# One-hot arrays of the expert routing: from whole-group two-array operations to per-query one-array operations on fixed engines

## The reference, cut to what matters

```python
q = (x @ w_pq).reshape(N, PEER_HEADS, 2, PEER_DQ_HALF)
s1 = einsum('nhd,kd->nhk', q[:, :, 0], k_sub1)      # 8 heads x 128 keys
s2 = einsum('nhd,kd->nhk', q[:, :, 1], k_sub2)
v1, i1 = top_k(s1, 16);  v2, i2 = top_k(s2, 16)
cand = v1[..., :, None] + v2[..., None, :]
sc, pos = top_k(cand, 16)
idx = take_along_axis(i1 * 128 + i2, pos)
wts = softmax(sc)
...
act = gelu(einsum('nhed,nd->nhe', u_exp[idx], x))
out = einsum('nhe,nhed->nd', wts * act, v_exp[idx])
```

## Time and profile before

| what | value |
|---|---|
| median of three runs | 5878.06 us |
| the profiled execution's own time | 5881.79 us |
| its span, first to last instruction | 5880.2 us |
| mean granted TensorE clock | 0.94 |
| TensorE busy | 5142.8 us (87%) |
| VectorE busy | 3439.7 us (58%) |
| ScalarE busy | 1786.7 us (30%) |
| GpSimd busy | 1495.8 us (25%) |
| compares on VectorE, L1933 | 48, 83.9 us |
| GpSimd's subtractions, L1786, and multiplies, L1797 | 48 each, 115.0 and 105.6 us |
| ScalarE's Abs, L1879, and Relu, L1883 | 48 each, 50.8 and 50.7 us |

### The profile page before, as it was taken

The page is one execution under the profiler, slowest core; times in us unless marked ns, Lnnn a source line. Parts: engine busy times, 40 slices in busy tenths (PEclk is TensorE's granted clock), DMA queues, the critical chain, the costliest instruction groups (busy, mean ns, idle before and its releaser), DMA issues. The chain is left out here.

```text
span 5880.2 us, 62559 instructions
## 1 busy us (share of the span) xinstructions
PE 5142.8 (87%) x23461; PEld 4166.5 (71%) x23461; DVE 3439.7 (58%) x4209; ACT 1786.7 (30%) x2132; POOL 1495.8 (25%) x1065
## 2 busy tenths in 40 slices
PE   8979999999998787989694449999999999978884
PEld 3347888888876334877573439999999899957673
DVE  7832211117663332222318777888888778878888
ACT  7743121222212111122314633333333223323332
POOL 0300000000000331000204642333333333344553
PEclk9989999999999898989896769999999999999997
DMA  9832322232323554432511449999999999999997
GB/s 357 308 129 92 107 98 87 96 109 99 111 81 117 176 199 148 159 110 84 161 65 49 101 134 362 386 367 384 373 379 380 369 373 377 377 383 408 402 410 312
DMA packets 467404, 1355.44 MB, mean 231 GB/s; under 512 B 137468, under 2 KB 194812, under 8 KB 383918
## 3 DMA queue, kind: packets, MB, share of 16 engines
q1 hardware_dynamic: 340500, 677.84, 32.8%
q0 software_dynamic: 99616, 633.82, 27.5%
q10 hardware_dynamic: 27072, 40.91, 2.0%
HBM read 1216.48 MB, written 137.04 MB: 230 GB/s over the span
## 5 line engine op out<-in xcount | busy, mean ns | idle before, releaser
L227 PE MATMUL ps<-w_hi,act_hi 128*128 128x512 f32 x3040 | 1196.8, 394 | 41.9 <-DVE act_lo L1032 23.0
L228 PE MATMUL ps<-w_lo,act_hi 128*128 128x512 f32 x3040 | 1191.1, 392 | 0.0
L229 PE MATMUL ps<-w_hi,act_lo 128*128 128x512 f32 x3040 | 1190.2, 392 | 0.0
L222 DVE TENSOR_TENSOR w_lo<-w_stage,w_hi 128x2048 fp32r<-128x2048 f32 x152 | 348.3, 2292 | 1270.3 <-ACT w_hi L218 1268.5
L2229 ACT ACTIVATE x_hi<-x_stage 128x1024 fp32r<-128x1024 f32 x512 | 543.5, 1061 | 1509.1 <-DMA x_stage<-u_turned 720.9
L2309 DVE TENSOR_TENSOR x_lo<-x_stage,x_hi 128x1024 fp32r<-128x1024 f32 x512 | 625.3, 1221 | 373.9 <-ACT x_hi L2229 369.4
L2156 POOL DMA_INDIRECT u_ring<-u_exp,idx_all x256 | 597.2, 2333 | 892.1 <-DVE u_ring L2327 833.3
L2183 PE MATMUL ps<-act_hi,x_hi 128*128 128x384 f32 x2048 | 697.8, 341 | 70.6 <-DVE x_lo L2309 67.9
L2183 PE MATMUL ps<-x_hi,cx_hi 128*128 128x512 f32 x1536 | 612.4, 399 | 101.0 <-DVE cx_lo L2320 84.1
L218 ACT ACTIVATE w_hi<-w_stage 128x2048 fp32r<-128x2048 f32 x152 | 291.1, 1916 | 1335.4 <-PE ps L229 1301.1
L2184 PE MATMUL ps<-act_lo,x_hi 128*128 128x384 f32 x2048 | 694.9, 339 | 0.0
(11 more groups left out here) (296 smaller groups left out, 5954.6 us busy)
## 6 DMA issues: line engine op xcount, KB each, us to landing
x_stage<-u_turned SPq DMA_DIRECT2D x256, 512.0 KB
x_stage<-v_exp SPq DMA_DIRECT2D x256, 512.0 KB
w_stage<-w_ada SPq DMA_DIRECT2D x96, 1024.0 KB, 6.1
w_stage<-w_in SPq DMA_DIRECT2D x96, 1024.0 KB, 5.2
d_w<-w_buf SPq DMA_DIRECT2D x6, 4096.0 KB, 20.7
gwr<-d_w SPq DMA_DIRECT2D x128, 192.0 KB
d_gw<-gob ACTq DMA_DIRECT2D x128, 192.0 KB
gwr<-d_gw SPq DMA_DIRECT2D x128, 192.0 KB
```

The source lines that it names most:

```text
L222: dve.tensor_tensor(w_lo[:, q % 2], w_in_st[:, q], w_hi[:, q % 2].bitcast(F32), ALU.subtract).then_inc(w_split, 1)
L227: pe.matmul(out, lhs[0], rhs[0], start=first, stop=False)
L228: pe.matmul(out, lhs[0], rhs[1], start=False, stop=False)
L229: return pe.matmul(out, lhs[1], rhs[0], start=False, stop=last)
```

## The change

An operation now makes the one-hot of a single token: `tensor_scalar` compares the numbers 0 to 127 (one array of 128 columns) with a number a partition, and for the second array multiplies by another number a partition. A group is 8 such calls. Who makes it is fixed by group number: of four groups, the first array is made by ScalarE, ScalarE, VectorE, GpSimd, the second by GpSimd, VectorE, VectorE, VectorE. Where ScalarE makes the first array it does eight Abs calls of 128 columns with the key as bias, and one Relu on 1024 columns. The subtraction and the multiplication on GpSimd are gone, with their semaphores; each engine has a semaphore of its own for the groups that it makes. one2's ring has four groups now, one1's still three. pij and pf are placed in an area that was free, dist has one buffer.

```diff
-    RING = 3
+    RING1, RING2 = 3, 4
     half = 4 * TT * KD * P
     spare = 4 * ND * KD * P
+    FIRST_BY = ("act", "act", "dve", "pool")
+    SECOND_BY = ("pool", "dve", "dve", "dve")
+
+    def makers(table, Q):
+
+        who = table[Q % len(table)]
+        return who, sum(table[n % len(table)] == who for n in range(Q + 1))
+
     at_sb = nc.alloc_sbuf_tensor_at
     qt = at_sb("qt", [P, NH, P], F32, offset=area + spare)
     q_t = at_sb("q_t", [P, NH, P], F32, offset=area + spare + 4 * NH * P)
     hot = at_sb("hot", [P, PH, TOPK, TOPK], F32, offset=area + half + spare)
-    dist = at_sb("dist", [P, 2, 8, P], F32, offset=area + half + spare + 4 * NH * P)
+    dist = at_sb("dist", [P, 8, P], F32, offset=area + half + spare + 4 * NH * P)
+    pij = at_sb("pij", [P, 4, PH, TOPK], U32, offset=area + half + spare + 4 * NH * P + 32 * P)
+    pf = at_sb("pf", [P, 4, PH, TOPK], F32, offset=area + half + spare + 4 * NH * P + 48 * P)
...
-        one1 = sb(st, "one1", [P, RING, 8, P])
-        one2 = sb(st, "one2", [P, RING, 8, P])
+        one1 = sb(st, "one1", [P, RING1, 8, P])
+        one2 = sb(st, "one2", [P, RING2, 8, P])
...
-        id_ready, id_taken, s_diff, s_dist, s_one1, s_eq2, s_one2 = (
-            sem("r_" + n) for n in ("idready", "idtaken", "diff", "dist", "one1", "eq2", "one2"))
+        id_ready, id_taken, s_dist = (sem("r_" + n) for n in ("idready", "idtaken", "dist"))
+        s_one1 = {who: sem("r_one1" + who) for who in ("act", "pool", "dve")}
+        s_one2 = {who: sem("r_one2" + who) for who in ("pool", "dve")}
...
-        def key_pairs(t, n, q):
-
-            return (iota.unsqueeze(1).broadcast_to([P, 8, P]),
-                    id_t[:, t % 2, n, 8 * q:8 * q + 8].unsqueeze(2).broadcast_to([P, 8, P]))
+        def first_hot(eng, who, Q):
+
+            if Q >= RING1:
+                eng.wait_ge(w_ready, 2 * (Q - RING1) + 2)
+            t, q = divmod(Q, NQ)
+            for j in range(8):
+                n = 8 * q + j
+                made = eng.tensor_scalar(one1[:, Q % RING1, j], iota, id_t[:, t % 2, 0, n:n + 1], None, ALU.is_equal)
+            made.then_inc(s_one1[who], 1)
+
+        def second_hot(eng, who, Q):
+
+            if Q >= RING2:
+                eng.wait_ge(w_ready, 2 * (Q - RING2) + 2)
+            t, q = divmod(Q, NQ)
+            for j in range(8):
+                n = 8 * q + j
+                made = eng.tensor_scalar(one2[:, Q % RING2, j], iota, id_t[:, t % 2, 1, n:n + 1],
+                                         id_t[:, t % 2, 2, n:n + 1], ALU.is_equal, ALU.mult)
+            made.then_inc(s_one2[who], 1)
...
-            def differ(t, q):
-                Q = t * NQ + q
-                if Q >= 2:
-                    pool.wait_ge(s_one1, Q - 1)
-                pool.tensor_tensor(dist[:, Q % 2], *key_pairs(t, 0, q), ALU.subtract).then_inc(s_diff, 1)
-
             for t in range(ND):
                 pool.wait_ge(id_taken, t + 1)
                 for q in range(NQ):
                     Q = t * NQ + q
-                    if q == 0:
-                        differ(t, 0)
-                    if q < NQ - 1:
-                        differ(t, q + 1)
-                    pool.wait_ge(s_eq2, Q + 1)
-                    pool.tensor_tensor(one2[:, Q % RING], one2[:, Q % RING],
-                                       id_t[:, t % 2, 2, 8 * q:8 * q + 8].unsqueeze(2).broadcast_to([P, 8, P]),
-                                       ALU.mult).then_inc(s_one2, 1)
+                    if makers(SECOND_BY, Q)[0] == "pool":
+                        second_hot(pool, "pool", Q)
+                    if makers(FIRST_BY, Q)[0] == "pool":
+                        first_hot(pool, "pool", Q)
...
-                pe.wait_ge(s_one1, Q + 1)
-                pe.wait_ge(s_one2, Q + 1)
+                who, made = makers(FIRST_BY, Q)
+                pe.wait_ge(s_one1[who], made)
+                who, made = makers(SECOND_BY, Q)
+                pe.wait_ge(s_one2[who], made)
                 for h in range(2):
                     G = 2 * Q + h
                     if G >= 2:
                         pe.wait_ge(w_taken, G - 1)
                     for j in range(4):
-                        mm = pe.matmul(ps[:, 6 + G % 2, j * P:(j + 1) * P], one1[:, Q % RING, 4 * h + j],
-                                       one2[:, Q % RING, 4 * h + j], start=True, stop=True)
+                        mm = pe.matmul(ps[:, 6 + G % 2, j * P:(j + 1) * P], one1[:, Q % RING1, 4 * h + j],
+                                       one2[:, Q % RING2, 4 * h + j], start=True, stop=True)
...
-                act.wait_ge(s_diff, Q + 1)
-                act.activation(dist[:, Q % 2], dist[:, Q % 2], ACT.Abs).then_inc(s_dist, 1)
-                act.wait_ge(s_dist, Q + 1)
-                if Q >= RING:
-                    act.wait_ge(w_ready, 2 * (Q - RING) + 2)
-                act.activation(one1[:, Q % RING], dist[:, Q % 2], ACT.Relu, scale=-1.0, bias=1.0).then_inc(s_one1, 1)
+                who, made = makers(FIRST_BY, Q)
+                if who != "act":
+                    return
+                if made > 1:
+                    act.wait_ge(s_one1["act"], made - 1)
+                for j in range(8):
+                    n = 8 * q + j
+                    act.activation(dist[:, j], iota, ACT.Abs, scale=-1.0,
+                                   bias=id_t[:, t % 2, 0, n:n + 1]).then_inc(s_dist, 1)
+                act.wait_ge(s_dist, 8 * made)
+                if Q >= RING1:
+                    act.wait_ge(w_ready, 2 * (Q - RING1) + 2)
+                act.activation(one1[:, Q % RING1], dist[:], ACT.Relu, scale=-1.0, bias=1.0).then_inc(s_one1["act"], 1)
...
                     t, q = divmod(Q, NQ)
                     if q == 0:
                         dve.wait_ge(id_taken, t + 1)
-                    if Q >= RING:
-                        dve.wait_ge(w_ready, 2 * (Q - RING) + 2)
-                    dve.tensor_tensor(one2[:, Q % RING], *key_pairs(t, 1, q), ALU.is_equal).then_inc(s_eq2, 1)
+                    if makers(FIRST_BY, Q)[0] == "dve":
+                        first_hot(dve, "dve", Q)
+                    if makers(SECOND_BY, Q)[0] == "dve":
+                        second_hot(dve, "dve", Q)
```

More of the change, by code:

```diff
@@ L1733, in route @@
         pos = sb(st, "pos", [P, PH, TOPK], U32)
-        pij = sb(st, "pij", [P, 4, PH, TOPK], U32)
-        pf = sb(st, "pf", [P, 4, PH, TOPK])
         step1 = sb(st, "step1", [P, PH, TOPK])
```

## The result

| what | before | after |
|---|---|---|
| median of seven runs (lowest to highest), us | 5867.74 (5855.97 to 5882.37) | 5834.27 (5829.05 to 5848.73) |
| ratio, 95% interval | | 0.9946 [0.9929, 0.9963] |
| routing, first MAX8 of tile 0 to SyncE's first load behind the stage, us | 396.1 (3103.07 to 3499.18) | 363.8 (3098.63 to 3462.44) |
| VectorE busy in that time, us | 342.1 | 326.4 |

About 32 us faster at the ratio's middle, 0.54%. The forecast was 5870 with a range from 5842: too high, and the faster rival (5843) came in, nearly 9 us beyond its own number. Of the 36 us between 5870 and 5834, 10 lie in the starting point: the forecast was counted from the 5878.06 of three runs, and seven runs of the kernel before give 5867.74. The rest is the change itself, forecast at 9 us and measured at 32. The two profiled executions lie 52.7 us apart (5881.79 and 5829.05).

The account below looks back on a forecast made before the run. VectorE's own program with its waits was taken to bound routing. Tiles 1 and 2 at 97.8 us against 102.5 and tile 3 at 93.5 against 93.0 gave -9 us together, 5870 us at the median; range 5842 to 5905.

Parts of the forecast that it names:

- the faster rival: GpSimd's 128-column calls hardly cost VectorE the port in routing: stalls about 4 us a tile, -35 us, 5843; chance 0.33.
- What bounds the kernel: Routing lasts as long as VectorE's own program with its waits; a microsecond on that path is one of the kernel.
- (1): VectorE in routing: 16 compares removed, -18.2 us a tile.
- (2): VectorE in routing: 12 second and 4 first groups of 8 small calls added, 31.4 us a tile.
- (3): VectorE's waits for spreading matmuls, exponential and tail: 5.8 us a tile instead of 19.0; tile 3, 1.3 instead of 7.4.
- (4): GpSimd gets 64 one-array calls a tile, taken at 0.50 us each: 32 us of work against 61 before.
- the slower rival: GpSimd's small calls are nearly all fixed cost, 0.8 to 0.9 us: at 0.92, +46 us, 5924; chance 0.23.
- d: The length of one GpSimd 128-column one-array call in routing, taken as 0.50 us; break-even at 0.57.
- S: VectorE's port stalls a tile in routing; the change is 3S-47 us and breaks even at S = 15.7.
- (5): VectorE's port stalls beside GpSimd's calls: 10.8 us plus 2 for hot operations, 12.8 us a tile instead of 17.5 to 19.4.
- (6): ScalarE's eight groups of Abs calls and a Relu take 29 us a tile against 34, and cost nothing.
- 43 pairs: The count per tile of VectorE small calls meeting a GpSimd call in routing, at 0.25 us each: 10.8 us.

Follow-up runs that it names:

- kernel 4: The changed kernel with GpSimd's groups made by VectorE too, so that GpSimd makes none: 5855.44 us, 0.9979.
- kernel 9: The changed kernel with group 12's second array made by VectorE and group 11's first by ScalarE: 5847.04 us, 0.9963.
- kernel 3: The kernel before, its VectorE compare made by eight one-number calls of 128 columns a group, GpSimd's two-array operations kept: 5888.0 us, 1.0029.
- kernel 2: The changed kernel with GpSimd's share made by two-array calls of 128 columns (its output is not one-hot): 5842.09 us, 0.9949.
- kernels 1 and 8: 1: kernel before, GpSimd's operations one-array, 512 columns, half of each group omitted, 5813.77 us; 8: changed kernel, earlier exponential, two group arrays moved, VectorE first arrays two-array, 5815.04 us.
- kernel 7: The changed kernel with ScalarE's exponential for the next tile issued behind the eviction of group 11 instead of group 13: 5813.41 us, 0.9904.

## Why the prediction was wrong, step by step

- **What bounds the kernel:** right. The stage still ends with VectorE's last routing instruction (SyncE's load at 3462.44), and its 32.3 us are the gain.
- **(1) and (2), the calls:** right. 0.266 and 0.206 us undisturbed in kernel 4 against 0.26 and 0.20, so 32.1 us a tile against 31.4, and more than the 18.2 of the compares.
- **(3), the waits:** half right. For the spreading matmuls 0 was forecast and 0.4 a tile came; for the tail 4.0 and 5.7, since not one but two groups of spreads are left there, one starting at 3230.96. For the exponential 1.8 (tile 3: 1.3) was forecast and 5.4 (4.7) came. The forecast took one GpSimd multiply out of the chain ahead of it, and forgot that VectorE, no longer stopped, arrives there earlier as well; kernel 9 showed that GpSimd isn't on that chain. Together +5.5 us in tile 1.
- **(4), GpSimd's call:** wrong, 0.60 and 0.83 us in place of 0.50. The forecast halved the 0.92 us of 256 columns, but 0.60 us at 128 columns and 1.56 at 512 are 2.5 ns a column and some 0.28 us that don't halve (an estimate), which gives 0.92 at 256. By the prediction's own rule this is the slower rival's ground: with d at their mean of 0.72, S = 43x0.47+2 = 22.2, and the kernel +20 us. It came out 32 us faster, which is the clearest sign that the rule and not a number failed.
- **(5), the port stalls: the step that failed.** "VectorE gets one call through per GpSimd call, so a pair costs VectorE d-0.25." Where it took 10.8 us a tile for the calls and 2 for hot, 1.7 were measured in the calls and 0.17 in the hot operations. The rows it rests on are true, and kernel 3 shows the same pattern again, but they are of a call that reads two arrays of 1024 columns, and such a call holds VectorE off until 0.14 us before its end. The length of a call and the time in which it holds VectorE off are nearly one number there, and the sum carried over the wrong one: a one-array call of 1024 columns lets VectorE go 1.88 us before its end, one of 128 columns 0.50 before. It reads for an estimated 128x0.75 = 0.1 us of its 0.6 to 0.8, so 43 pairs could cost 4 us. As a cross-check, also an estimate from the same rate: columns times arrays times 0.75 ns gives 147 us for GpSimd's calls before (96 calls), 55 in kernel 2 (288 calls) and 18 after (192 calls), of which VectorE lost 54, 18 and 5: 37, 32 and 28%.
- The Trainium skill's rule that was set beside (5) (page "SBUF — State Buffer", section "Who interferes with whom") says that the two engines exclude each other for whole instructions. The runs here agree where the engine that is ahead reads two arrays: GpSimd's two-array calls hold VectorE until 0.14 us before their end, and VectorE's two-array operations of 2.29 us stretch single GpSimd calls of 0.78 to 3.03 and 2.67. They don't agree for GpSimd's one-array calls, which let VectorE go 0.50 to 1.88 us before their end. The Trainium skill's other sentence, on roughly line-rate GpSimd work (page "GPSIMD Engine Reference", section "Engine selection"), led to the right side by a wrong number: the calls weren't the estimated 0.27 us but 0.6 to 0.8.
- **(6), ScalarE:** right. The Abs calls take 58.1/192 = 0.30 us from start to start, and VectorE waited at its rings for 1.3 us in all.
- **The rivals.** The faster one had the right mechanism, "a GpSimd call of 128 columns may hold the port for a small part of its time", with a chance of 0.33. The evidence for it, an early stage where GpSimd's call gave way to VectorE, was weighed below the rows nearest in kind, though those differ from the new call in both size and arrays. That its own -35 us lies so near the measured -32 is in part luck: its 4 us of stalls a tile were too many, and its waits, those of the forecast, 14 us too few.

The sum by measured terms for tile 1: 47.7 + 32.6 (calls and stalls) + 11.3 (waits) = 91.6, against 90.7 measured; 0.9 us of tile 0's own idle time is covered in tile 1.

What stays open: the two small forms' delays, 0.15 and 0.13 us, are too short to tell the rate at 128 columns, and the difference of the two profiled runs behind the routing stage stays unexplained.

## What to carry to other kernels

When GpSimd slows VectorE, count what GpSimd reads (columns times arrays), not how long it is busy: one-array calls with numbers per partition are slower on GpSimd itself and still take far less from VectorE. GpSimd's half is the one that pays: small VectorE calls beside large two-array GpSimd calls lose (kernel 3), while VectorE's large two-array compares pass GpSimd's one-array calls almost undelayed (1242 and 1236 ns, kernels 1 and 8). GpSimd's half alone, in a kernel that computes the right thing, wasn't run. And after stalls are gone, look at the waits again at once, since the engine that is now early meets an order made for a late one; moving one exponential by two groups (kernel 7, 5813.41 us, the best found) took another 16 us off the stage, half of what the change itself gave.

## What the runs showed of the hardware

- GpSimd's call of one array is slower than that of two at the same columns: 0.60 (one number) or 0.83 (two numbers) against 0.40 us at 128 columns, 1.56 against 1.04 at 512, 2.85 against 1.9 at 1024.
- A call of two arrays holds a VectorE operation that starts behind it until 0.14 us before its end, at 1024, 512 and 128 columns; a call of one array lets it go 1.88, 1.03 and 0.50 us before its end. The greatest delays are 1.58, 0.72 and 0.15 us against 0.80, 0.37 and 0.13.
- In the other direction VectorE's two-array operations of 2.29 us hold GpSimd off: single calls of 0.78 us took 3.03 and 2.67, and eight took 12.23 us instead of 6.7. Three calls inside a VectorE reduction of 2.27 us, which reads one array, took 0.78 each.
- Each number per partition adds 0.06 to 0.07 us to VectorE's 128-column call: 0.137 (immediates, on integers), 0.206, 0.266 us from start to start.
